# A coarse level's decays in sixteen biased passes: moving work from VectorE to ScalarE inside a chunked recurrence

## The reference, cut to what matters

```python
b = jnp.cumsum(gc, axis=2)
inter = jnp.einsum('bhtk,bhkv->bhtv', qc * jnp.exp(b), s)
diff = b[:, :, :, None, :] - b[:, :, None, :, :]
decay = jnp.where(causal, jnp.exp(jnp.minimum(diff, 0.0)), 0.0)
scores = jnp.einsum('bhtk,bhtsk,bhsk->bhts', qc, decay, kc)
intra = jnp.einsum('bhts,bhsv->bhtv', scores, vc)
s_new = jnp.exp(b_last) * s + einsum(kc * jnp.exp(b_last - b), vc)
```

## Time and profile before

| what | value |
| --- | --- |
| time, median of 3 runs | 2651.73 us (2648.08 to 2653.44) |
| profiled execution, its own time | 2651.76 us |
| span of that execution | 2650.0 us |
| TensorE, VectorE, ScalarE busy | 2509.8, 1619.4, 962.1 us |
| mean granted clock of TensorE | 0.981 |
| recurrence | from about 1340 to 1800 us of the span |

### The profile page before, as it was taken

The page is one execution under the profiler, slowest core; times in us unless marked ns, Lnnn a source line. Parts: engine busy times, 40 slices in busy tenths (PEclk is TensorE's granted clock), DMA queues, the critical chain, the costliest instruction groups (busy, mean ns, idle before and its releaser), DMA issues. The chain is left out here.

```text
span 2650.0 us, 39415 instructions
## 1 busy us (share of the span) xinstructions
PE 2509.8 (95%) x16737; PEld 1347.5 (51%) x16737; DVE 1619.4 (61%) x2109; ACT 962.1 (36%) x1116; POOL 26.8 (1%) x60
## 2 busy tenths in 40 slices
PE   7989789999999999999899999989979999999997
PEld 4457564444444444443577676764434444444443
DVE  6688747544444443645467878786766766774253
ACT  5127307432323231423255646562432222222121
POOL 0000000020000000000000000000000000000000
PEclk9999899999999999999899999999989999999998
DMA  9027464112111123433100001022101111213332
GB/s 327 24 89 233 152 209 143 32 33 63 47 47 47 48 81 104 113 107 127 52 25 25 25 19 30 17 80 64 32 16 48 47 47 51 60 53 104 110 107 88
DMA packets 302919, 207.38 MB, mean 78 GB/s; under 512 B 11296, under 2 KB 298174, under 8 KB 302143
## 3 DMA queue, kind: packets, MB, share of 16 engines
q1 hardware_dynamic: 301910, 205.08, 25.8%
q10 hardware_dynamic: 873, 0.32, 0.0%
HBM read 191.22 MB, written 13.64 MB: 77 GB/s over the span
## 5 line engine op out<-in xcount | busy, mean ns | idle before, releaser
L200 PE MATMUL ps<-hT,arena 128*128 128x512 bf16 (+1 forms) x6240 | 1345.9, 378 | 27.4 <-DVE arena L2084 9.9
L200 PEld LDWEIGHTS ps<-hT,arena 128*128 128x128 bf16 x6240 | 611.5, 98 | 759.3 <-issue 42.7
L1905 PE MATMUL ps<-arena 128*128 128x512 bf16 x2112 | 458.8, 379 | 2.6 <-DVE arena L1887 2.5
L1905 PEld LDWEIGHTS ps<-arena 128*128 128x128 bf16 x2112 | 206.2, 98 | 252.0 <-DVE arena L1887 5.0
L2157 DVE SCALAR_TENSOR_TENSOR arena<-ps,vec,arena 128x945 f32<-128x945 f32 (+2 forms) x176 | 215.1, 1222 | 76.0 <-ACT arena L2143 56.6
L2124 DVE SCALAR_TENSOR_TENSOR arena<-ps,vec,arena 128x1023 f32<-128x1023 f32 (+1 forms) x88 | 106.7, 1275 | 179.7 <-ACT arena L2114 179.7
L1887 DVE TENSOR_TENSOR arena<-hT,arena 128x2816 bf16<-128x2816 f32 (+2 forms) x44 | 93.7, 2156 | 158.9 <-ACT arena L1881 158.8
L1881 ACT ACTIVATE arena<-hT 128x2816 bf16<-128x2816 f32 (+2 forms) x44 | 77.8, 1798 | 237.3 <-DMA hT<-w_down_dram 109.9
L2943 PE MATMUL ps<-arena 128*128 128x128 f32 x896 | 109.7, 279 | 18.3 <-DVE arena L3256 12.8
L2071 DVE TENSOR_TENSOR arena<-hT,arena 128x2048 bf16<-128x2048 f32 x44 | 100.9, 2292 | 28.2 <-ACT arena L2038 27.9
L2943 PEld LDWEIGHTS ps<-arena 128*128 128x128 f32 x896 | 105.2, 194 | 21.9 <-DVE arena L3256 20.0
(11 more groups left out here) (436 smaller groups left out, 2550.2 us busy)
## 6 DMA issues: line engine op xcount, KB each, us to landing
xT<-ada_w_dram SPq DMA_DIRECT2D x24, 1024.0 KB, 5.3
hT<-w_up_dram SPq DMA_DIRECT2D x44, 512.0 KB, 4.9
hT<-ffn_up_dram SPq DMA_DIRECT2D x44, 512.0 KB, 5.1
hT<-w_down_dram SPq DMA_DIRECT2D x30, 704.0 KB, 7.0
hT<-ffn_down_dram SPq DMA_DIRECT2D x30, 704.0 KB, 6.8
arena<-w_in_dram SPq DMA_DIRECT2D x33, 512.0 KB, 4.0
xT<-w_mod_dram SPq DMA_DIRECT2D x16, 1024.0 KB, 5.9
arena<-w_mod_dram SPq DMA_DIRECT2D x8, 1024.0 KB, 19.2
```

What stands on the lines that cost most here:

```text
L200: last = pe.matmul(out, lhs(a, kt), rhs(b, kt, i), start=start and kt == 0 and (a, b) == (0, 0), stop=stop and kt == n_k - 1 and (a, b) == ...
L1905: last = pe.matmul(self.bank(u), self.part(u, a, kt), self.g[:, b, kt, cols], start=kt == 0 and (a, b) == (0, 0), stop=kt == FT - 1 and (a ...
```

## The change

Level 0 (halves of 64 tokens) loses its subtraction on VectorE. ScalarE makes its decays straight from `b`: it negates the 8 middles into a new small tile `minus_mid`, then runs 16 passes of 64 columns, each an exponential with the middle of its chunk as bias (scale -1 and the middle for the keys, scale 1 and the negated middle for the queries). They signal a semaphore of their own, `first_exp`, so the counts of `sub_done` and `exp_done` become 6 a unit. These passes stand at the end of `query_decays`; the pass of level 1 moves from there behind the take-out of `kt`.

TensorE's product of level 0 uses the key half of each chunk as its weights and the query half as its columns, so it writes 64 rows and 64 columns of the 128 by 128.

On VectorE, `weigh` of level 0 is followed by `diagonal`, `weigh` of level 1 and `select` of level 0; `subtract` of level 2 comes behind these, `select` of level 1 ahead of `subtract` of level 3. The weight splits `weights_lo` for GATE and QUERY move from the end of a unit to a place behind `weigh` of level 2 of the next one.

```diff
+    minus_mid = take(T // P)
...
             def level(n, l):
                 pe.wait_ge(x_ready, NL * n + l + 1)
                 v = x[:, buffer(n, l), :]
-                chunk_job((n, "level", l), range(T // P), lambda out, c: pe.matmul(
-                    out, v[:, c * P:(c + 1) * P], v[:, c * P:(c + 1) * P], start=True, stop=True))
+                d, m = units[n][1], LEVELS[l]
+                whole = 2 * m < P
+                rows = slice(0, P) if whole else slice(d * m, (d + 1) * m)
+                columns = slice(0, P) if whole else slice((1 - d) * m, (2 - d) * m)
+
+                def product(out, c):
+                    chunk = v[:, c * P:(c + 1) * P]
+                    return pe.matmul(out[rows, columns], chunk[:, rows], chunk[:, columns], start=True, stop=True)
+
+                chunk_job((n, "level", l), range(T // P), product)
...
+            def first_level(n):
+
+                if n > last_unit:
+                    return
+                d, m = units[n][1], LEVELS[0]
+                logs, v = x_tokens(b[:, n % 2, :]), x[:, buffer(n, 0), :]
+                mid = lambda c: logs[:, c * P + m - 1 + d:c * P + m + d]
+                mids = logs.rearrange("p (c r) -> p c r", r=P)[:, :, m - 1 + d]
+                act.wait_ge(b_ready, n + 1)
+                if n:
+                    wait_made(act, (n - 1, "level", NL - 3))
+                link(act.activation(minus_mid, mids, ACT.Copy, scale=-1.0))
+                for c in range(T // P):
+                    keys_at = slice(c * P + d * m, c * P + (d + 1) * m)
+                    queries_at = slice(c * P + (1 - d) * m, c * P + (2 - d) * m)
+                    act.activation(v[:, keys_at], logs[:, keys_at], ACT.Exp, scale=-1.0, bias=mid(c))
+                    last = act.activation(v[:, queries_at], logs[:, queries_at], ACT.Exp, bias=minus_mid[:, c:c + 1])
+                last.then_inc(first_exp, 1)
+
             def level(n, l):
-                act.wait_ge(sub_done, NL * n + l + 1)
+                act.wait_ge(sub_done, (NL - 1) * n + l)
...
                 act.activation(z, z, ACT.Exp).then_inc(kh_exp, 1)
-                level(n, 0)
...
                 act.activation(qh, x_tokens(bn), ACT.Exp).then_inc(qh_exp, 1)
-                level(n, 1)
+                first_level(n)
...
                 signal((n, "kt", 1), kt_done)
+                level(n, 1)
                 if d == 0 and h:
                     squares(h - 1)
...
-                dve.wait_ge(exp_done, NL * n + l + 1)
+                if l:
+                    dve.wait_ge(exp_done, (NL - 1) * n + l)
+                else:
+                    dve.wait_ge(first_exp, n + 1)
...
             key_distance(0)
-            subtract(0, 0)
...
                 weigh(n, 0)
-                subtract(n, 2)
                 diagonal(n)
                 weigh(n, 1)
                 select(n, 0)
+                subtract(n, 2)
+                select(n, 1)
                 subtract(n, 3)
                 weigh(n, 2)
-                select(n, 1)
+                if n:
+                    weights_lo(n, GATE)
+                    weights_lo(n, QUERY)
                 subtract(n, 4)
...
                 if d == 1:
-                    subtract(n + 1, 0)
                     weights_lo(n + 1, V1)
...
                 if d == 0:
-                    subtract(n + 1, 0)
                     subtract(n + 1, 1)
-                weights_lo(n + 1, GATE)
                 scale_q(n + 1)
-                weights_lo(n + 1, QUERY)
```

## The result

The changed kernel takes 2656.85 us (median of 20 runs, 2651.07 to 2662.85), the kernel before 2650.61 in runs beside it: a ratio of 1.0023, 95% interval 1.0016 to 1.003, so 6 us slower. The forecast was 2656.6 us. That the two times lie 0.3 us apart is partly luck: the forecast added 4.85 us to a median of three runs, 2651.73, while the movement against the 20 runs beside it is 6.2 us. At 0.23% this lies just over the 0.2% at which the prediction drew its line: it called no change the likeliest, and slower came next.

What follows compares the result with a forecast made beforehand. TensorE, busy 95% of the span, was taken to bound the kernel. Odd units -6.3, even units +7.95, unit 0 -0.5, unit 7 +1.3 and the clock +2.4 gave +4.85: 2656.6 us, range 2649.5 to 2662.

Steps and rivals of the forecast that it cites:

- the 0.2% at which the prediction drew its line: Whole kernel: a measurement tells about 0.2%, 5.3 us, from no change; between those bounds the chance was 0.55.
- A pass: ScalarE, level 0's decays: a biased exponential of 64 columns takes 0.24 us start to start.
- the ends (0.155, 0.33): Rival pass times on ScalarE: 0.155 us overlapping, 2650.2 us, chance 0.12; 0.33 without overlap, 2660.1 us, chance 0.08.
- Odd units: Units 1, 3, 5: level 0 starts without its wait and level 1 sooner; gain 2.1 us each, 6.3 in three.
- Unit 0 and unit 7: First and last units: the first gains 0.5 us by an earlier diagonal, the last loses 1.3 by later final steps.
- Half products: TensorE, level 0 on half the columns: ends before level 1 may start, so worth nothing in odd or even units.
- Even units, without the clock: Units 2, 4, 6: late passes delay level 1 and z0 comes later; loss 2.65 us each, 7.95 in three.
- The second wait: Even units: z0 waits about 1.6 us for banks that ScalarE's inverse root frees, behind level 3's decays.
- The clock: Even units: TensorE's granted clock falls after idle stretches, partly on level 1; 0.8 us each, 2.4 in three.
- the first rival: Clock falls fully on level 1 of each even unit, perhaps odd ones too: 2659.2 or 2664.1 us, chance 0.25.
- the 1.2 us that the moved split was to give: Even units: the preceding tile's lower half moves up, so the weight's DMA lands and qh starts 1.2 us earlier.
- The sum: Whole kernel: all terms together +4.85 us, of which +2.45 without a clock fall; 2656.6 us, chance 0.50.

Runs made afterwards that it cites:

- full_columns: Changed kernel with level 0's product whole again, all 128 by 128; ratio 1.0008 to the kernel before.
- root_first: Changed kernel with the inverse root ahead of level 3's decays on ScalarE; ratio 1.0016 to the kernel before.
- early_passes: Changed kernel with the 16 passes of even units moved ahead of the query's bf16 weight copy and qh; ratio 0.9999 to the kernel before.
- early_both: Changed kernel with even units' passes early, level 2's subtraction before level 0's weighing, level 1's selection behind level 2's weighing; ratio 0.9985 to the kernel before.
- double_passes: Changed kernel with 32 passes of 32 columns in place of 16 of 64; ratio 1.0127 to the kernel before.
- old_order: Changed kernel, passes kept, with VectorE's first steps back in the order of before; ratio 1.0035 to the kernel before.

## Why the prediction was right, point by point

- A pass: 0.24 us taken, 0.240 measured; the row of a biased exponential of 256 columns was the right one, although what followed it there was the reading of an accumulator and not another exponential, and the ends (0.155, 0.33) played no part. The Trainium skill (ScalarE: Activation LUTs, What ACT_TABLE_LOAD costs) gives the same, 0.24, an estimate from its figures for a pointer as bias; the trace agrees.
- Odd units: -2.1 forecast, -2.14 to -2.15 measured, by the steps named: level 0 without a wait, level 1 behind the diagonal. Unit 0 and unit 7 came out within 0.1 us.
- Half products are worth nothing here: full_columns shows it in odd units. In units 2 and 4 of the profiled executions they even cost a little, through the clock.
- Even units, without the clock: +2.65 forecast, 1.0 because level 1 is late and 1.65 because z0 then waits for the root. Measured in units 2, 4 and 6, level 1 is late by 1.84, 1.13 and 0.83 us, and the root adds 1.85, 1.85 and 1.82. The second wait is there and ended by the root's logarithm; root_first took it away. That unit 6, the one without a low clock at level 1, comes to +2.65 is luck: its diagonal product was late at a low clock, level 0 waited 0.74 us behind it and not 1.95, and a smaller first part met a larger second one.
- The clock: the step that was mis-sized. It was to cost 0.8 us in each of three even units, 2.4; in units 2 and 4 level 1 needed 3.58 us to the next product instead of 1.89, so 1.7 in each of two, 3.4, the upper bound, and nothing at level 1 in unit 6. For units 2 and 4 the first rival, a clock that falls fully on level 1, was right; for unit 6 and the odd units it was not. The Trainium skill (TensorE: Matmul & The Clock Gate, Why this matters for your kernels) warns of longer gaps only; here the clock fell behind gaps of 2.73 and 2.02 us, each before a product of about 1.2 us and another gap.
- One thing was wrong by 0.85 us: in unit 2 the weight's DMA landed later. Split's end to copy was 3.9 us in the earlier trace rows, and 4.77 here (1465.28 to 1470.05), so most of the 1.2 us that the moved split was to give was lost, level 0 waited 2.73 us instead of 1.95, and level 1 came at 7.20 us instead of 6.35. Why it landed later is not shown; in unit 4 the same stretch took 4.05 us. With it and 1.7 of the clock unit 2 is explained to 0.2 us (2.65 + 0.85 + 1.7 = 5.2 of 5.38).
- The sum was +4.85; the profiled units give +7.1, the runs +6.2. The clock (1.0 more), the late DMA (0.85) and the root (0.6 more in three units) account for the 2.25 between; smaller differences take 0.2 off.

## What to carry to other kernels

Work moved to an engine with idle time is only free where that engine has nothing ahead of it and nobody queues behind: the same 16 passes ended in odd units before TensorE needed what is made of them, and in unit 2 3.9 us after VectorE had asked for them. When an order is changed, look at who frees the banks of the next large job, not only at the operands; here a logarithm of another head held a projection. Order was worth more than the arithmetic: with the inputs of levels 0 and 1 made first, 11 us came without the passes, and the passes and half products then added another 9, of which the half products were about half; in the order in which they were first tried, the change as a whole cost 6.

## What the runs showed of the hardware that was not expected

The clock does not follow from the length of one gap. Windows of 1 us, unit 2, early_passes and then early_both (length, busy share and records, granted clock, DMA share, GB/s), both behind an idle stretch of 1.80 us and the same work before it:

```profile
1483.00:1484.00 1.00, 1.00 (x11) 1.00 0.06 16
```

```profile
1483.00:1484.00 1.00, 1.00 (x7) 0.50 0.09 16
```

In early_passes it stayed at 1.00 in units 2 and 4, in early_both it fell to 0.50 in units 2, 4 and 6. Units 3 and 5 of double_passes are such a pair inside one execution. At 1.2 GHz sixteen matmuls of level 1 took up to 3.58 us to the next product instead of 1.89, and where the result is on the path that is 1.7 us. Changes of 2 or 3 us in this kernel can therefore be undone or doubled by where the clock falls: old_order and double_passes missed their expectations by 5 and 10 us, for the most part in this way. What decides it in a single gap stays open.
